# Two layer norms moved into the blocks behind them, a first pair of slabs taken chunk by chunk, a residual flipped in the experts' block, single steps ahead of double ones

## The chip, the core and the metric

The kernel runs on one core of a Trainium2 chip, as one program. The metric is the device time in microseconds (us) of an execution, the median of the runs. TensorE (PE in the profile) multiplies, VectorE (DVE) and ScalarE (ACT) work elementwise, GpSimd (POOL) does elementwise work and gathers, SyncE (SP) and ACT issue DMAs.

## The reference

Tokens are 512 rows of width 1024. A first block (attention, a convolution, a product-key expert layer) is followed by a second block of two layers, and only the second block is touched:

```python
for layer in range(2):
    sh1, sc1, g1, sh2, sc2, g2 = jnp.split(cond @ ada_w[layer] + ada_b[layer], 6, axis=-1)
    u = x * (1.0 + sc1) + sh1
    mix = _mixer(u, ...)                    # u @ w_in, short conv, gated linear attention, @ w_out
    x = _layernorm(ALPHA * x + (1.0 + g1) * mix, ln1_g[layer], ln1_b[layer])
    u = x * (1.0 + sc2) + sh2
    ff = _dense_swiglu(u, ...) if layer == 0 else _moe_swiglu(u, ...)   # 8 experts, top 2
    x = _layernorm(ALPHA * x + (1.0 + g2) * ff, ln2_g[layer], ln2_b[layer])
```

A layer norm subtracts the mean over the 1024 channels, divides by the root of the mean square plus 1e-5, and applies a gain and a bias.

## The kernel before

`x` lies with channels on the partitions: 8 chunks (`KT`) of 128 channels by 512 tokens. `self.h` holds the modulated input `u`, `self.squares` is a scratch tile of the same size. Every stage is a block of its own: all engines meet at its end. PSUM is eight banks, `bank` (four, for products) and `side` (four).

Products are made precise by splitting float32 operands in a rounded part and a rest: three matmuls for one. A weight slab of 128 output channels comes by DMA into a ring of four slots; ACT rounds it (`round_slab`, L249, two buffers, so slab i waits until slab i-2 is used), GpSimd subtracts (`split_slabs`, L257), and `fine` (L278) makes 8 chunks x 3 matmuls. The input is split the same way, ACT rounding (`round_source`, L267) and DVE subtracting (`split_source`, L272), chunk by chunk; the first slab waits for each chunk (`ready`).

`normalise` (L309) is a block: DVE centres with a mean that TensorE summed with a matrix of ones, ACT squares, TensorE sums the squares, ACT takes the root, DVE the reciprocal (L354) and scales (L357), and ACT makes `x` and then `h` of each chunk (L343). It stands after the residual of layer 0 (L2611, ahead of `dense_up`) and after `dense_down` (L2634, ahead of the second `mix_in`). The first has its mean from `residual` (L1649), which adds the chunks on DVE (L1689) and sums the result once on TensorE (L1663); the second makes eight mean matmuls itself (L365). `route` (L1828), behind the second residual, has its norm built in: gain and modulation are folded in `s.fold` (L1934 to L1936), so that `h` comes straight from the scaled `x` (L1913) and `x` gets its own gain and bias later (L1917).

`mix_in` (L1410) starts with a low-rank product of `h` with 16 columns (L1425), whose result ACT copies (L1463) ahead of its loop over slabs; then 24 slabs. `dense_up` (L1696) makes 44 slabs. `dense_down` (L1751) makes 16 wide ones, while DVE makes dot products of modulation rows (L397) that ACT fetches, and at its end the modulation's gains (`second_gains`).

`route` picks two experts for each token, turns `h` to rows (`flip`, L1859) and stores them as `token_rows`, and turns and stores ALPHA times `x` as `kept_x` (L1905, L1849), which `finish` reads back. `run_experts` (L2050) runs 15 blocks of 128 token slots as 4 double steps (two blocks of one expert) and 7 single ones. Each step streams the 33 slabs (1 MB each) of its expert, with 11 ring slots and 3 rounded buffers; some ring slots lie over `h`, `squares` and `x`. A block's rows are gathered by GpSimd into the one tile `s.xs` (L2120), turned by TensorE (L2138) and split by DVE in two halves (L2269, L2271); the next gather waits until this block is turned. Order of steps: four times (double, single), then three singles (`tail`). Two blocks are turned ahead of the loop, the others within steps (`flips`). SP issues slabs in order; the one of index `kept_over` (5), whose slot lies over `kept_x`'s source, waits for the stores.

## Time and profile before

| | us |
|---|---|
| median of 3 runs | 4841.65 (4836.25 to 4850.41) |
| the profiled run | 4848.16 |
| its span | 4846.3 |
| TensorE busy | 4079.7 (84%) |
| VectorE busy | 2875.5 (59%) |
| ScalarE busy | 1662.4 (34%) |
| GpSimd busy | 1418.9 (29%) |

The profile is one execution. The second block starts near 2280 us and the experts' loop at 3327 us. A busy share is an average over stages; each idle time is read with what ended it (`<-`). The granted clock of TensorE has two levels, shown as 1.00 (2.4 GHz) and 0.50 (1.2 GHz).

### The profile page before, as it was taken

The page shows a single profiled execution, that of the slowest core. Times are in us where ns is not written, and L with a number is a line of the kernel's source. Part 1 is how long each engine was busy: PE and PEld are TensorE (multiplying, and loading weights), DVE is VectorE, ACT ScalarE, POOL GpSimd, SP SyncE. Part 2 cuts the span into 40 slices and gives each one's busy share as a digit, 9 for nine tenths or more (in the row PEclk, how much of TensorE's full clock was granted, in tenths as well). Part 3 has the DMA queues.
Part 4 walks back from the last instruction along what each step waited for, and adds up shares of the span by engine and source line. Part 5 has one row for each costly group of instructions (what it writes and reads, how often), then busy time and mean ns, then how long its engine had stood idle before and what let it go on. Part 6 is the DMA issues. An engine that isn't in the chain of part 4 may idle for free. (4 is left out here: it accounts for less than half of the span.)

```text
span 4846.3 us, 43572 instructions
## 1 busy us (share of the span) xinstructions
PE 4079.7 (84%) x14930; PEld 2725.5 (56%) x14930; DVE 2875.5 (59%) x4171; ACT 1662.4 (34%) x2193; POOL 1418.9 (29%) x1231
## 2 busy tenths in 40 slices
PE   4988997986776766767978998977999999999995
PEld 3864543432322322323756875755878777787774
DVE  4886656565655665652364365454475664747886
ACT  2222402221211212212314323323364554646775
POOL 0430003666666666664413442310000000000000
PEclk7998998998999999999988999988999999999998
DMA  4225086999999999995312263206585765857995
GB/s 151 96 82 199 1 278 251 372 374 362 370 367 367 364 371 366 373 369 213 96 40 70 95 232 124 84 18 247 187 332 189 265 252 194 327 190 296 354 361 199
DMA packets 260053, 1147.99 MB, mean 237 GB/s; under 512 B 28832, under 2 KB 28832, under 8 KB 212512
## 3 DMA queue, kind: packets, MB, share of 16 engines
q0 software_dynamic: 150768, 549.00, 29.7%
q1 hardware_dynamic: 87792, 516.46, 29.5%
q10 hardware_dynamic: 21312, 80.15, 4.5%
q8 instruction: 110, 1.80, 0.1%
q14 instruction: 71, 0.58, 0.0%
HBM read 1131.33 MB, written 14.16 MB: 236 GB/s over the span
## 5 line engine op out<-in xcount | busy, mean ns | idle before, releaser
L1340 PE MATMUL psum<-row,diag 128*128 128x512 f32 x1632 | 802.4, 639 | 297.5 <-DMA row<-in_peer_v,expert 124.3
L1340 PEld LDWEIGHTS psum<-row,diag 128*128 128x128 f32 x1632 | 316.8, 203 | 771.7 <-issue 505.1
L1171 DVE CUSTOM_DVE_ANT_0 row<-row,psum 128x1024 f32<-128x1024 f32 x412 | 497.4, 1219 | 309.7 <-DMA row<-in_peer_u,expert 213.6
L1138 POOL DMA_INDIRECT row<-in_peer_u,expert x412 | 392.7, 953 | 561.9 <-DVE expert L1084 425.8
L2159 PE MATMUL psum<-exp_high,exp_xt 128*128 128x512 f32 x1320 | 527.3, 400 | 28.4 <-DVE exp_low L2275 17.3
L2159 PE MATMUL psum<-exp_high,exp_xlow 128*128 128x512 f32 x1320 | 517.7, 392 | 0.0
L2159 PE MATMUL psum<-exp_low,exp_xt 128*128 128x512 f32 x1320 | 515.7, 391 | 0.0
L1138 POOL DMA_INDIRECT row<-in_peer_v,expert x408 | 385.7, 945 | 255.8 <-issue 121.2
L1252 ACT ACTIVATE diag<-consts_sb,coef 128x128 f32<-128x128 f32 x512 | 175.2, 395 | 591.2 <-PE psum L1340 229.7
L2117 POOL COPY exp_number<-moe_slot_token 128x1 uint32 (+1 forms) x15 | 7.2, 482 | 1211.7 <-PE psum L2138 1155.9
L2159 PEld LDWEIGHTS psum<-exp_high,exp_xt 128*128 128x128 f32 x1320 | 248.9, 189 | 83.3 <-DVE exp_low L2275 17.4
L2159 PEld LDWEIGHTS psum<-exp_high,exp_xlow 128*128 128x128 f32 x1320 | 248.6, 188 | 53.9
L2159 PEld LDWEIGHTS psum<-exp_low,exp_xt 128*128 128x128 f32 x1320 | 249.2, 189 | 49.2
L2183 PE MATMUL psum<-exp_high,exp_ht 128*128 128x512 f32 x660 | 261.4, 396 | 13.2 <-DVE exp_htlow L2286 13.2
L2275 DVE TENSOR_TENSOR exp_low<-exp_wring,exp_high 128x2048 fp32r<-128x2048 f32 x99 | 225.3, 2291 | 75.9 <-ACT exp_high L2215 74.4
L2183 PE MATMUL psum<-exp_high,exp_htlow 128*128 128x512 f32 x660 | 261.2, 396 | 0.0
L2183 PE MATMUL psum<-exp_low,exp_ht 128*128 128x512 f32 x660 | 260.7, 395 | 0.0
L2215 ACT ACTIVATE exp_high<-exp_wring 128x2048 fp32r<-128x2048 f32 x99 | 188.4, 1913 | 56.3 <-PE psum L2183 46.9
L262 POOL TENSOR_TENSOR mix_low<-slab_ring,mix_high 128x1024 fp32r<-128x1024 f32 x48 | 119.3, 2486 | 237.6 <-ACT mix_high L255 237.6
L618 DVE SCALAR_TENSOR_TENSOR psum<-gpad,vectors_sb,psum 128x512 f32<-128x512 f32 x240 | 181.4, 756 | 8.6
L2275 DVE TENSOR_TENSOR exp_low<-slab_ring,exp_high 128x2048 fp32r<-128x2048 f32 x66 | 151.3, 2292 | 54.1 <-ACT exp_high L2215 53.5
L2275 DVE TENSOR_TENSOR exp_low<-h,exp_high 128x2048 fp32r<-128x2048 f32 x66 | 150.3, 2292 | 49.5 <-ACT exp_high L2215 49.0
(464 smaller groups left out, 8007.8 us busy)
## 6 DMA issues: line engine op xcount, KB each, us to landing
exp_wring<-in_moe SPq DMA_DIRECT2D x99, 1024.0 KB, 6.1
h<-in_moe SPq DMA_DIRECT2D x66, 1024.0 KB, 6.0
squares<-in_moe SPq DMA_DIRECT2D x66, 1024.0 KB, 6.5
x<-in_moe SPq DMA_DIRECT2D x66, 1024.0 KB, 6.6
slab_ring<-in_moe SPq DMA_DIRECT2D x66, 1024.0 KB, 5.8
slab_ring<-in_w_in SPq DMA_DIRECT2D x92, 512.0 KB
mix_rows<-in_ada ACTq DMA_DIRECT2D x48, 512.0 KB, 5.2
squares<-in_ada ACTq DMA_DIRECT2D x48, 512.0 KB, 6.4
```

What stands on the lines that cost most here:

```text
L262: pool.tensor_tensor(s.low[:, i % 2, :], self.ring[(base + i) % SLOTS][:, 0:D], s.high[:, i % 2, :].bitcast(F32), ALU.subtract).then_inc(s ...
L618: dve.scalar_tensor_tensor(sum_, gp[:, tap:tap + T], self.vec("conv_w", TAPS * c + tap), sum_, ALU.mult, ALU.add).then_inc(tapped.sem, 1)
L1138: pool.indirect_dma_start(out=s.row[row % ROWS], out_offset=None, in_=table, in_offset=bass.IndirectOffsetOnAxis(ap=s.expert[:, g, j:j + 1 ...
L1171: dve.tensor_tensor_reduce(at, at, tokens[g // PH], 1.0, 0.0, ALU.mult, ALU.add, s.act[:, g % 2, j:j + 1]).then_inc(row_used.sem, 1)
L1252: act.activation(s.diag[:, number % DIAGS, :], self.const("ident"), ACT.Copy, scale=s.coef[:, g % 2, j:j + 1]).then_inc(lined.sem, 1)
L1340: mm = pe.matmul(sums[:, half * T:(half + 1) * T], s.diag[:, (PTOP * g + j) % DIAGS, :], s.row[row % ROWS][:, half * T:(half + 1) * T], st ...
L2117: pool.tensor_copy(s.number[:], s.slot_token[:, ds(place, 1)]).then_inc(numbered.sem, 1)
L2159: mm = pe.matmul(self.bank[:, buffers(of, c).start + u, :], xx[:, part * KT // 2 + k, :], w[:, at], start=part == 0 and k == 0 and n == 0, ...
L2183: mm = pe.matmul(self.side[:, 2 * u + half, :], x[:, m, kk * P:(kk + 1) * P], w[:, at], start=c == 0 and kk == 0 and n == 0, stop=c == STE ...
L2215: act.activation(s.high[:, i % ROUNDED, :], s.wring[i % MOE_SLOTS], ACT.Copy).then_inc(rounded.sem, 1)
L2275: dve.tensor_tensor(s.low[:, i % ROUNDED, :], s.wring[i % MOE_SLOTS], s.high[:, i % ROUNDED, :].bitcast(F32), ALU.subtract).then_inc(split ...
```

## The change

- The two `normalise` blocks of the second block are gone. `dense_up` and the second `mix_in` do the norm themselves, as `route` does: folded gains, `h` and its rounded part both made by ACT from the scaled `x` (`norm_act`), DVE centring, scaling and splitting (`norm_dve`), TensorE summing the squares (`norm_pe`). ACT rounds the first two slabs ahead of it. `x` gets its gain and bias within the loop over slabs.
- The first two slabs are multiplied together, chunk by chunk (`fine_pair`); slabs 2 and 3 follow (`fine_rest`). In the second `mix_in` the low-rank product comes between them.
- `dense_down` sums `x` as `residual` does and calls `second_gains` ahead of its last wait.
- `route` no longer turns and stores `kept_x`; `run_experts` does at its start, with the stores on ACT's queue.
- In `run_experts` each pair of steps is (single, double), one block is turned ahead of the loop, and the first tail turns two.

```diff
+    def norm_act(self, act, s, eps, scale, bias):
+        for k in range(KT):
+            act.wait_ge(centred.sem, centred.at(k + 1))
+            act.activation(self.squares[:, k, :], self.x[:, k, :], ACT.Square).then_inc(squared.sem, 1)
+        act.wait_ge(summed.sem, summed.at(1))
+        act.activation(self.stat[:, 0, :], self.side[:, 0, :], ACT.Sqrt, bias=self.eps[eps], scale=1.0 / D).then_inc(rooted.sem, 1)
+        for k in range(KT):
+            act.wait_ge(scaled.sem, scaled.at(k + 1))
+            act.activation(self.h[:, k, :], self.x[:, k, :], ACT.Identity, scale=scale(k), bias=bias(k)).then_inc(normed.sem, 1)
+            act.activation(s.hhigh[:, k, :], self.x[:, k, :], ACT.Identity, scale=scale(k), bias=bias(k)).then_inc(rounded.sem, 1)
...
+    def norm_dve(self, dve, s, gain, bias, scale, shift):
...
+        for k in range(KT):
+            dve.scalar_tensor_tensor(self.x[:, k, :], self.side[:, 1, :], -1.0 / D, self.x[:, k, :], ALU.mult, ALU.add).then_inc(centred.sem, 1)
...
+        for k in range(KT + 1):
+            if k < KT:
+                dve.tensor_tensor(self.x[:, k, :], self.x[:, k, :], self.stat[:, 1, :], ALU.mult).then_inc(scaled.sem, 1)
+            if k:
+                dve.wait_ge(normed.sem, normed.at(k))
+                dve.wait_ge(rounded.sem, rounded.at(k))
+                dve.tensor_tensor(s.hlow[:, k - 1, :], self.h[:, k - 1, :], s.hhigh[:, k - 1, :].bitcast(F32), ALU.subtract).then_inc(split.sem, 1)
...
+    def fine_pair(self, pe, s):
...
+        pe.wait_ge(split.sem, split.at(2))
+        for k in range(KT):
+            pe.wait_ge(h_split.sem, h_split.at(k + 1))
+            at = slice(k * P, (k + 1) * P)
+            for slot in range(2):
+                for n, (w, x) in enumerate(((s.high, s.hhigh), (s.low, s.hhigh), (s.high, s.hlow))):
+                    mm = pe.matmul(self.bank[:, slot, :], w[:, slot, at], x[:, k, :], start=k == 0 and n == 0, stop=k == KT - 1 and n == 2)
+                if k == KT - 1:
+                    mm.then_inc(self.slab_used, 1)
...
@@ mix_in
+                if layer:
+                    self.norm_pe(pe)
+                    self.fine_pair(pe, s)
...
                 mm.then_inc(low.sem, 1)
-                self.slabs(pe, 0, SLOTS, self.fine(pe, s))
+                if layer:
+                    self.fine_rest(pe, s)
+                else:
+                    self.slabs(pe, 0, SLOTS, self.fine(pe, s))
...
+                    if layer and SLOTS < i <= SLOTS + KT:
+                        k = i - SLOTS - 1
+                        act.activation(self.x[:, k, :], self.x[:, k, :], ACT.Identity, scale=gain(k), bias=bias(k))
@@ dense_up
-                self.slabs(pe, 0, SLOTS, self.fine(pe, s))
+                self.norm_pe(pe)
+                self.fine_pair(pe, s)
+                self.fine_rest(pe, s)
...
-                self.round_source(act, s, self.h)
+                self.norm_act(act, s, LN_EPS, lambda k: s.fold[:, 0, k:k + 1], lambda k: s.fold[:, 1, k:k + 1])
@@ dense_down
+                pe.wait_ge(x_summed.sem, x_summed.at(KT - 1))
+                pe.matmul(self.side[:, 1, :], self.const("ones"), s.sum[:], start=True, stop=True).then_inc(averaged.sem, 1)
...
+                    if i == KT - 1:
+                        self.second_gains(dve, 1)
...
+                        dve.tensor_tensor(s.sum[:], s.sum[:] if i > 1 else self.x[:, 0, :], self.x[:, i, :], ALU.add).then_inc(x_summed.sem, 1)
@@ run_experts
-            return dict(step=2 * i, doubles=i, width=2, block=3 * i, place=[2 * i, 2 * i + 1], ring=[0, 1], flips=[(3 * i + 2, 2)])
+            return dict(step=2 * i + 1, doubles=i, width=2, block=3 * i + 1, place=[2 * i, 2 * i + 1], ring=[1, 2], flips=[(3 * i + 3, 0)])
...
+            return dict(step=2 * i, doubles=i, width=1, block=3 * i, place=[2 * DOUBLES + i], ring=[0],
+                        flips=[(3 * i + 1, 1), (3 * i + 2, 2)])
...
+                for t in range(TT):
+                    act.wait_ge(x_copied.sem, x_copied.at(TT + t + 1))
+                    act.dma_start(s.kept_x[t * P:(t + 1) * P, :], s.xn[:, t, :]).then_inc(x_kept.sem, 16)
                 for i in range(AHEAD):
                     round_slab(0, i)
...
-                for n in range(2):
-                    for half in range(2):
-                        x_half(n, n, half)
-                for i in range(AHEAD):
+                split_slab(0, 0)
+                for half in range(2):
+                    x_half(0, 0, half)
+                for i in range(1, AHEAD):
                     split_slab(0, i)
```

## Rows read from the trace of the kernel before

**Rows 1.** Windows (from:to and length, busy us and count per engine, clock, DMA, GB/s).
```profile
2529.90:2566.60 36.70, 10.80 (x19) 4.18 (x19) 16.87 (x22) 21.96 (x32) 3.02 (x2) 0.64 0.05 15
...
3327.60:4795.00 1467.40, 1424.27 (x6374) 1159.31 (x6374) 970.53 (x656) 791.91 (x634) 18.35 (x24) 1.00 0.71 262
```

**Rows 2.** Timeline (start us, us, engine, line, operation, idle before), join A.
```profile
2533.68 4.88 DVE L351 SCALAR_TENSOR_TENSOR x<-psum,x 128x512 f32<-128x512 f32 x8 [1.50 <-PEq L1653]
...
2535.09 9.64 PE L371 MATMUL psum<-squares,consts_sb 128*128 128x512 f32 x16 [1.73 <-ACT squares L330]
...
2545.48 3.35 DVE L354 RECIPROCAL stat<-stat 128x512 f32<-128x512 f32 x1 [6.93 <-ACT stat L332]
...
2576.85 1.06 ACT L255 ACTIVATE ffn_high<-slab_ring 128x1024 fp32r<-128x1024 f32 x1 [8.24 <-PE psum L290]
...
2577.99 2.40 POOL L262 TENSOR_TENSOR ffn_low<-slab_ring,ffn_high 128x1024 fp32r<-128x1024 f32 x1 [9.28 <-ACT ffn_high L255]
```

**Rows 3.** Timeline, the folded gains and the h activations in `route`.
```profile
3240.30 0.17 DVE L1934 TENSOR_TENSOR route_fold<-vectors_sb,cooked 128x8 f32<-128x8 f32 x1 [1.50 <-PEq L1653]
...
3256.49 5.77 ACT L1913 ACTIVATE h<-x,route_fold 128x512 f32<-128x512 f32 x8 [4.21 <-DVE x L1946]
```

**Rows 4.** Forms of one line (duration ns min/median/max, first to last start).
```profile
L276 DVE TENSOR_TENSOR ffn_hlow<-h,ffn_hhigh x8: 678/680/2866, 2565.0 to 2572.2; 128x512 fp32r<-128x512 f32 x8
...
L1689 DVE TENSOR_TENSOR res_sum<-res_sum,x x12: 691/2762/2762, 2503.5 to 3238.1; 128x512 f32<-128x512 f32 x12
...
L618 DVE SCALAR_TENSOR_TENSOR psum<-gpad,vectors_sb,psum x240: 755/756/760, 138.3 to 355.7; 128x512 f32<-128x512 f32 x120
```

**Rows 5.** Timeline, end of `dense_down` and start of the second `mix_in`.
```profile
2949.93 0.75 DVE L1813 TENSOR_SCALAR stat<-psum,cooked 128x512 f32<-128x512 f32 x1 [1.37 <-PE psum L1773]
...
2987.52 8.60 PE L1425 MATMUL psum<-h,small_sb 128*16 128x512 f32 x16 [17.74 <-PEq L321]
...
3002.01 1.06 ACT L255 ACTIVATE mix_high<-slab_ring 128x1024 fp32r<-128x1024 f32 x1 [5.27 <-PE psum L290]
...
3007.59 1.06 ACT L255 ACTIVATE mix_high<-slab_ring 128x1024 fp32r<-128x1024 f32 x1 [4.03 <-PE psum L290]
```

**Rows 6.** Timeline, end of `route` and start of `run_experts`.
```profile
3287.58 6.38 PE L1859 MATMUL psum<-consts_sb,x 128*128 128x128 f32 x32
...
3289.47 0.17 DVE L2025 CAST moe_slot_token<-psum 128x16 uint32<-128x16 f32 x1
...
3292.55 2.89 SPq L1849 DMA_DIRECT2D kept_x<-squares  x4
...
3295.91 0.20 ACT L2209 ACTIVATE exp_mark<-eps 128x1 f32<-128x1 f32 x1 [1.31 <-PEq L1841]
...
3297.24 0.99 POOL L2120 DMA_INDIRECT exp_xs<-token_rows,exp_number  x1 [0.77 <-POOL exp_number L2117]
...
3302.93 1.91 ACT L2215 ACTIVATE exp_high<-exp_wring 128x2048 fp32r<-128x2048 f32 x1 [6.82 <-DMA exp_wring<-in_moe]
...
3305.76 1.12 PE L2138 MATMUL psum<-consts_sb,exp_xs 128*128 128x128 f32 x4 [11.79 <-DMA exp_xs<-token_rows,exp_number]
...
3320.12 1.11 PE L2138 MATMUL psum<-consts_sb,exp_xs 128*128 128x128 f32 x4 [10.56 <-DMA exp_xs<-token_rows,exp_number]
...
3327.63 0.79 PE L2159 MATMUL psum<-exp_high,exp_xt 128*128 128x512 f32 x1 [3.71 <-DVE exp_low L2275]
```

**Rows 7.** Windows (columns as in Rows 1), most of the first double step.
```profile
3335.00:3420.00 85.00, 83.59 (x380) 68.50 (x380) 42.01 (x29) 33.51 (x25) 1.15 (x2) 1.00 0.53 188
```

**Rows 8.** Windows of TensorE alone: busy, clock, DMA share, GB/s.
```profile
3327.60:3332.00 4.40, 4.37 (x10) 0.50 1.02 425
...
3577.70:3581.20 3.50, 3.50 (x10) 0.52 0.96 405
```

**Rows 9.** Timeline, TensorE waits for a gather inside single steps.
```profile
3577.14 0.65 PE L2138 MATMUL psum<-consts_sb,exp_xs 128*128 128x128 f32 x4 [2.66 <-DMA exp_xs<-token_rows,exp_number]
...
4456.02 0.65 PE L2138 MATMUL psum<-consts_sb,exp_xs 128*128 128x128 f32 x4 [0.94 <-DMA exp_xs<-token_rows,exp_number]
```

141 lines of the change are left out of this document (90 added, 51 removed).

## The prediction

> **What bounds the kernel now.** I read the windows of the two long stretches first. In the experts' loop TensorE is busy 1424 of 1467 us at full clock, so nothing the other engines save inside the loop is worth anything; only when it starts, and what TensorE waits for in it, counts [rows 1]. In the first join, from the last product of the residual to the first of the dense layer, TensorE is busy 10.8 of 36.7 us at a mean clock of 0.64 [rows 1]. The change works on three such joins, called A (into `dense_up`), B (into the second `mix_in`) and C (into `run_experts`). In the timelines the reader is to follow which engine releases which.
>
> **Join A, the chain before.** Centring starts at 2533.68, the sum of squares takes TensorE 9.64 us because its clock is low at first, Sqrt takes 0.75 us between the sum and the reciprocal, the reciprocal 3.35 [rows 2]; then scaling and sixteen activations, a block end, two slab roundings, the split of h, and products from 2566.6 [rows 1]. Slab 0 is used at 2576.85 and slab 1 a slab time of 5.58 later (the spacing of the two roundings in [rows 5]), so slab 2 starts at 2582.4.
>
> **Join A, after.** The block starts at the same 2533.7. DVE folds gains (three operations of 0.17, 0.5 with gaps [rows 3]) and centres. ACT has two slab roundings ahead of its squares (1.06 each by [rows 2], 2.0), so the first square starts at 2535.7 and the TensorE sum some 0.7 later, 2536.4; with 9.64 it ends 2546.1. Sqrt 0.75 and reciprocal 3.35 give 2550.2. Then the first chunk passes scale 0.68, two activations at 0.72 spacing (eight in 5.77, [rows 3]) and the subtraction 0.68 [rows 4], about 3.1 with latencies: the pair begins at 2553.3. Later chunks come every 1.45 to 1.5 us (two activations; DVE needs 1.3), below the 2.56 that six matmuls take at low clock and near the 1.40 at full clock (5.58/24 each). 48 matmuls: about 10 in 4.4 us at low clock, as at the loop's start [rows 8], and 38 x 0.2325 = 8.8; end 2566.5. The moved affine of x (eight times 0.72) lies on ACT beside 5.58 us slabs of which ACT uses under 3: cost nothing; without that cover it would be 0.7 per chunk. The split of h loses its one blocked operation (2.87 against 0.68, [rows 4]), since GpSimd is done by then; that is already in the sum.
>
> Something is given back. Both slabs of the pair finish within three matmuls, and slab 2's rounding waits for slab 0's use, at 2565.8: rounding and split take 3.54 (2576.85 to the end of the GpSimd row, [rows 2]), so slab 2 starts at 2569.5 and TensorE idles 3.0. A wait of 2.66 in the loop was followed by 3.5 us at half clock [rows 8, 9], a loss of 1.75; I take 1.8 here, between 0 and 2.2. A = 2582.4 - 2569.5 - 1.8 = **11.1 us**.
>
> **Join B.** Before, slab 1 of `mix_in` is used at 3007.6 [rows 5]. After, `dense_down` sums x itself: seven DVE additions and one TensorE product in place of eight matmuls. The additions are on an engine that waits for TensorE at the end (1.37, [rows 5]). One that overlaps GpSimd takes 2.76 instead of 0.69 [rows 4], but now the row dot that was caught there is not, so each costs 0.7; `second_gains` (five operations on a few columns, 0.6 by the 0.17 of [rows 3] with overlap) moves ahead of the last wait, and what is queued behind it is the last x chunk. 1.37 covers 0.7 + 0.6; without the cover up to 1.5. From the last product to centring I take join A's 2533.7 - 2529.9 = 3.8: block start 2953.6. The same 19.6 to the pair gives 2973.2, and 13.2 more 2986.4. Then comes the low-rank product, now behind the pair: 8.60 before, partly at low clock; sixteen passes at 0.427 are 6.8, so I take 6.9 (ends 6.8 and 8.6). The ACT wait for it stands ahead of `next_slab(0)`, so queued behind it are its copy (0.6), the rounding of slab 2 and GpSimd's split: 2993.3 + 0.6 + 3.54 + 0.1 = 2997.5. Gain 10.1, less 2.2 for the clock after 4.2 idle (4.4 at half speed, [rows 8]): B = **7.9 us**.
>
> **Join C.** The route block loses eight transposed tiles, their copies and four stores. It ended with ACT, whose idle of 1.31 began at 3294.6; now DVE's cast at 3289.47 + 0.17 ends it [rows 6]: 5.0 sooner. Everything in the new block shifts so: the gather is issued at 3292.2 and, with the first one's 8.5 (3297.24 to the flip that waited for it at 3305.76), lands at 3300.7. TensorE flips x first (6.38, ACT ending 7.0 after its start [rows 6]) from 3290.9 to 3297.9, beside the wait for the gather. ACT then issues four stores (at most 0.72 each by SP's row, which holds waits for copies [rows 6]; 1.7 taken) and rounds slab 0 at 3299.7, which arrives at 3302.93 - 5.0 = 3297.9. Queued behind these waits on ACT are the first three roundings; on SP the slab of index 5 and everything behind it wait until the stores have landed. DVE splits slab 0 (2.3) to 3304.0, then does two halves of block 0, with a flip between, by 3308.2. TensorE starts there instead of at 3327.63, which waited for a second gather until 3320.12 [rows 6]: 19.4. At 425 GB/s [rows 8] a 1 MB slab takes 2.5 us and the stores' 2 MB take 5.0; slab 5 is issued by 3308.5, lands by 3316 and is wanted at about 3322, so this wait is hidden by 6 us. The single step lasts about 99 us (33 slabs x 12 products x 0.2325 = 92, and transposes), near 3.0 a slab, slower than 2.5, so a ring that starts empty holds. One block's flips move from ahead of the loop into the first tail: two flips of 0.6, plus a gather wait of 0 to 2.66 and the clock after it [rows 9]; I take the wait of 0.94 at 4456, the nearest row in time and in DMA load: 2.1 in all. C = 19.4 - 2.1 = **17.3 us**. With the stores' 5.0 lost, a wait of 2.66 and its 1.75 of clock it is 8.8, without any wait 18.2.
>
> The Trainium skill's SBUF page ("SBUF — State Buffer", section "SBUF: two separate sides") says that a DVE operation with two SBUF inputs and a GpSimd operation that reads SBUF lock each other out for a whole instruction. It speaks against the added additions in `dense_down`, and the trace agrees (0.69 or 2.76, [rows 4]). By it centring, which has one input in PSUM, would escape GpSimd's two splits, as the rows of L618 show (755 to 760 ns beside GpSimd). The page on DMA ("DMA: Bandwidth & Descriptors", section "Queues, rings and completion order") says that queues take turns by packet. By that, the stores on ACT's queue halve the slabs' rate for 10 us; slab 2 would come at 3308.7 and be split by 3313, where TensorE wants it at 3315.8, so the sum stays. No run here shows those two queues so loaded.
>
> **The sum.** 11.1 + 7.9 + 17.3 = 36.3 us. The profiled run took 4848.16, its span is 4846.3, so the changed one's should be near 4811.9 and 4810.0. The median of the three runs is 6.5 lower, 4841.65, which gives **4805.4 us**.
>
> **Rivals.** (1) Locks and clock eat the joins. GpSimd's two splits (5.1) now run beside centring; if they block it, 5.1 is lost in each join, and if low clock lasts twice its 4.4, since TensorE works with gaps there, 2.2 more. A is 3.8, B 0.6: 21.7 in all, 4820.0. Against it: L618 [rows 4]. (2) The experts' start collides: the stores hold back slab 0 or the gather by their full 5.0, and the first tail pays a full wait and half clock, 2.66 + 1.75. C is 8.8, the sum 27.8, time 4813.9. For it: ACT's 6.82 wait for slab 0 [rows 6] shows that it comes little before it is wanted. (3) The pair doesn't pay: chunk order only moves the wait to slab 2 and to the low-rank product. Then each join saves eight activations (5.7) and C its block end (5.0): 16.4, 4825.3. (4) Slower: the first step, a single one on an empty ring, is bound by slabs. In the first double step DMA moved 188 GB/s [rows 7]; at that rate 33 slabs take 184 us instead of 99, which is +85.1 - 36.3 = +48.8, 4890.5. It cancels the gain from 255 GB/s down. Against it: that rate was what the ring asked for (DMA share 0.53); before it the rate was 425.
>
> **Chances.** Forecast 0.63 (its own range 4796 to 4814), (1) 0.15, (2) 0.13, (3) 0.05, (4) 0.04. The bounds of the terms give gains of 3.8 + 0.6 + 8.8 = 13.2 up to 12.9 + 10.1 + 18.2 = 41.2, 4800 to 4828; the three runs spread over 14 us, so I set 4794 to 4826. About 0.3% (14.5 us) is what a measurement of this kernel can tell from none. Faster 0.88 (a bit of (1) to (3) falls past 4827), same 0.08, slower 0.04.
>
> **What would show it.** In A the first product of the pair at 2553, slab 2 at 2569 to 2571, an idle of 3 us ahead of it with GpSimd's split as its releaser, then half clock for some 4 us. In B the low-rank product starting near 2986 and an idle of 4 behind it. In C the first expert matmul 18.6 us behind route's last cast where it was 38.0, one gather ahead of it, SP waiting for the stores, no ACT wait for slabs after the third. A first step over 105 us, or centring with a 2.8 us operation, would prove (4) or (1); a gather wait over 2 us in the first tail, (2).

## The result, and the profile after

The changed kernel takes 4803.63 us (median of 5 runs, 4799.84 to 4813.17) where the kernel before takes 4841.65: ratio 0.9923, 95% interval 0.9907 to 0.9939, or 38.0 us less. The forecast was 4805.4. The profiled run took 4799.84, its span is 4798.0. The two profiled spans differ by 48.3, but 12.6 of that had been gained ahead of the first changed line (the last product of the residual ends at 2517.4 where it ended at 2530.0, in code that is the same), so the profiles are compared stretch by stretch. Each is one execution, and the next section shows which stretches come out otherwise in other profiles. In the changed kernel the norm's lines are L390 to L425, the pair L438, the low-rank product L1498, the single flip of `x` L2291.

| stretch, us | before | after | gain | forecast |
|---|---|---|---|---|
| A: residual's last TENSOR_SCALAR to the first rounding of `dense_down` | 290.6 | 279.8 | 10.8 | 11.1 |
| `dense_down`, to its last TENSOR_SCALAR | 129.4 | 129.5 | -0.1 | 0 |
| B: from there to the second residual's last TENSOR_SCALAR | 286.7 | 276.2 | 10.5 | 7.9 |
| `route`: from there to its last cast | 52.9 | 52.8 | 0.1 | 0 |
| C: cast to the first expert matmul | 38.2 | 18.7 | 19.5 | 19.4 |
| experts' loop, to its last copy from PSUM | 1467.9 | 1472.5 | -4.6 | -2.1 |

Windows of the changed kernel (from:to and length, busy us and count per engine, clock, DMA share, GB/s): join A up to the pair, the pair with the idle behind it, the start of slab 2, the start of slab 2 in join B, and the loop. They answer to [rows 1, 8].

```profile
2517.40:2541.70 24.30, 11.84 (x18) 4.36 (x19) 12.79 (x19) 9.29 (x15) 4.70 (x2) 0.69 0.07 22
2541.70:2558.70 17.00, 13.98 (x48) 10.84 (x48) 8.32 (x13) 12.84 (x17) 2.34 (x1) 0.83 0.14 47
2558.70:2562.70 4.00, 3.96 (x17) 3.27 (x18) 2.50 (x1) 1.52 (x3) 2.40 (x1) 1.00 0.18 69
2973.70:2977.30 3.60, 3.59 (x9) 2.91 (x10) 3.53 (x3) 0.00 (x0) 2.63 (x1) 0.54 0.02 5
3274.40:4746.40 1472.00, 1429.37 (x6382) 1163.20 (x6382) 972.72 (x660) 791.62 (x634) 20.61 (x27) 0.99 0.71 267
```

Before, 36.7 us passed from the residual to the first product; now it is 24.3. The third and fourth windows each stand behind an idle time of TensorE, and they differ: full clock in A, 0.54 in B.

The timeline of join A after the change (start us, us, engine, line, operation, idle before and its releaser), for [rows 2]:

```profile
2522.11 4.87 DVE L407 SCALAR_TENSOR_TENSOR x<-psum,x 128x512 f32<-128x512 f32 x8
2524.30 10.09 PE L425 MATMUL psum<-squares,consts_sb 128*128 128x512 f32 x16 [2.88 <-ACT squares L390]
2535.14 3.35 DVE L409 RECIPROCAL stat<-stat 128x512 f32<-128x512 f32 x1 [8.17 <-ACT stat L392]
2541.71 0.77 PE L438 MATMUL psum<-ffn_hhigh,ffn_high 128*128 128x512 f32 x1 [7.33 <-DVE ffn_hlow L418]
2555.12 1.06 ACT L255 ACTIVATE ffn_high<-slab_ring 128x1024 fp32r<-128x1024 f32 x1 [4.08 <-PE psum L438]
2556.25 2.34 POOL L262 TENSOR_TENSOR ffn_low<-slab_ring,ffn_high 128x1024 fp32r<-128x1024 f32 x1 [28.70 <-ACT ffn_high L255]
2558.74 0.47 PE L290 MATMUL psum<-ffn_hhigh,ffn_high 128*128 128x512 f32 x1 [3.05 <-POOL ffn_low L262]
```

ACT can't round slab 2 before the pair has used slab 0, at 2555.1; then ACT and GpSimd take 3.5 us, and TensorE idles 3.05 of it. Join B shows the same with the low-rank product and its copy ahead of the rounding, for [rows 5]:

```profile
2962.54 7.04 PE L1498 MATMUL psum<-h,small_sb 128*16 128x512 f32 x16
2969.61 0.59 ACT L1542 ACTIVATE low_rank<-psum 16x512 f32<-16x512 f32 x1 [10.99 <-PE psum L1498]
2970.11 1.04 ACT L255 ACTIVATE mix_high<-slab_ring 128x1024 fp32r<-128x1024 f32 x1
2971.22 5.11 POOL L262 TENSOR_TENSOR mix_low<-slab_ring,mix_high 128x1024 fp32r<-128x1024 f32 x2 [34.73 <-ACT mix_high L255]
2973.71 0.50 PE L290 MATMUL psum<-mix_hhigh,mix_high 128*128 128x512 f32 x1 [4.14 <-POOL mix_low L262]
```

The experts' start, for [rows 6]: one gather ahead of the first matmul, and SP's slab issues, which stop at 3260.4 for the stores issued by ACT at 3262.9 and go on only at 3281.86.

```profile
3255.70 0.17 DVE L2111 CAST moe_slot_token<-psum 128x16 uint32<-128x16 f32 x1
3257.72 0.98 POOL L2208 DMA_INDIRECT exp_xs<-token_rows,exp_number  x1 [0.78 <-POOL exp_number L2205]
3260.10 0.33 SPq L2191 DMA_DIRECT2D h<-in_moe  x1
3262.88 3.02 ACTq L2352 DMA_DIRECT2D kept_x<-squares  x4
3268.13 1.11 PE L2226 MATMUL psum<-consts_sb,exp_xs 128*128 128x128 f32 x4 [5.29 <-DMA exp_xs<-token_rows,exp_number]
3274.41 0.79 PE L2247 MATMUL psum<-exp_high,exp_xt 128*128 128x512 f32 x1 [1.60 <-DVE exp_xlow L2372]
3281.86 0.92 SPq L2191 DMA_DIRECT2D squares<-in_moe  x2
```

What nobody forecast is at the edge of the loop. With single steps first, the end of each double step and the start of the next single step lie on the two sides of the edge. The first edge:

```profile
3574.64 0.59 ACT L2318 ACTIVATE cond_rows<-psum 128x512 f32<-128x512 f32 x1
3576.21 1.28 ACT L2337 ACT_TABLE_LOAD   x1 [0.98 <-ACT cond_rows L2318]
3577.78 3.70 ACT L2309 ACTIVATE exp_high<-h 128x2048 fp32r<-128x2048 f32 x2
3582.07 0.80 PE L2247 MATMUL psum<-exp_high,exp_xt 128*128 128x512 f32 x1 [3.03 <-DVE exp_low L2376]
```

ACT loads a function table at the head of the loop body, and the rounding behind it is what TensorE waits for through DVE. The waits at the three edges are 3.03, 3.02 and 2.85, and each is followed by about half clock (windows of TensorE alone: busy, clock, DMA share, GB/s):

```profile
3582.00:3585.50 3.50, 3.43 (x9) 0.57 0.61 208
3875.20:3878.70 3.50, 3.42 (x8) 0.52 0.64 220
4168.60:4172.10 3.50, 3.41 (x8) 0.51 0.56 208
```

### The profile page after: what moved, and what is told of

Its sections match the earlier page's. It is cut to its first block and busy times, and to the rows that moved or that the text cites. A ratio compares the mean times of both kernels' runs of the same rounds, so it can differ in the third digit from the quotient of the medians.

```text
span 4798.0 us, 43540 instructions
## 1 busy us (share of the span) xinstructions
PE 4081.0 (85%) x14916; PEld 2727.2 (57%) x14916; DVE 2873.6 (60%) x4184; ACT 1659.6 (35%) x2193; POOL 1416.2 (30%) x1231
## 5 line engine op out<-in xcount | busy, mean ns | idle before, releaser
L2271 PE MATMUL psum<-exp_high,exp_ht 128*128 128x512 f32 x660 | 261.5, 396 | 13.2 <-DVE exp_htlow L2387 13.2
L1410 PE MATMUL psum<-stat,diag 128*128 128x512 f32 x204 | 116.5, 699 | 83.0 <-DMA stat<-in_peer_v,expert 39.4
L2376 DVE TENSOR_TENSOR exp_low<-slab_ring,exp_high 128x2048 fp32r<-128x2048 f32 x66 | 151.2, 2291 | 52.9 <-ACT exp_high L2309 52.3
```

What stands on the lines that cost most here:

```text
L1410: mm = pe.matmul(sums[:, half * T:(half + 1) * T], s.diag[:, (PTOP * g + j) % DIAGS, :], s.row[row % ROWS][:, half * T:(half + 1) * T], st ...
L2271: mm = pe.matmul(self.side[:, 2 * u + half, :], x[:, m, kk * P:(kk + 1) * P], w[:, at], start=c == 0 and kk == 0 and n == 0, stop=c == STE ...
L2376: dve.tensor_tensor(s.low[:, i % ROUNDED, :], s.wring[i % MOE_SLOTS], s.high[:, i % ROUNDED, :].bitcast(F32), ALU.subtract).then_inc(split ...
```

## The experiments

The twelve kernels ran on three chips, whose own medians of the kernel before are 4717.86 (e1 to e4), 4850.24 (e5 to e8) and 4857.41 (e9 to e12). Times are compared within a chip; no profile of the kernel before was taken on any of the three, so its stretches are those of the table above and, where a kernel leaves them as they were, those of e1 to e3. The stretches were read in each profile (d: `dense_down`, to its last TENSOR_SCALAR; r: `route`, to its last cast):

| kernel | median, ratio (interval) | A | d | B | r | cast to first matmul | loop |
|---|---|---|---|---|---|---|---|
| e1 join A only | 4707.81, 0.9976 (0.9966 to 0.9987) | 277.7 | 129.4 | 286.1 | 52.8 | 38.2 | 1474.4 |
| e2 join B only | 4708.85, 0.998 (0.9969 to 0.999) | 290.3 | 130.6 | 276.6 | 53.7 | 38.6 | 1474.9 |
| e3 join C only | 4694.91, 0.9946 (0.9929 to 0.9963) | 289.3 | 129.2 | 286.5 | 52.8 | 18.1 | 1473.8 |
| e4 slabs one by one | 4685.80, 0.9928 (0.9911 to 0.9944) | 277.6 | 130.2 | 281.7 | 55.9 | 18.6 | 1476.0 |
| e5 the change again | 4815.18, 0.9929 (0.9913 to 0.9946) | 278.9 | 130.6 | 276.6 | 53.7 | 18.9 | 1473.5 |
| e6 series, early rounding | 4814.38, 0.9923 (0.9907 to 0.994) | 277.6 | 130.9 | 274.5 | 55.9 | 18.7 | 1474.7 |
| e7 loop written out | 4806.86, 0.9908 (0.9891 to 0.9924) | 277.6 | 130.3 | 278.0 | 52.9 | 18.4 | 1469.6 |
| e8 double steps first | 4822.72, 0.9948 (0.9931 to 0.9964) | 278.9 | 130.2 | 276.9 | 54.9 | 32.6 | 1467.3 |
| e9 low-rank wait later | 4813.99, 0.9915 (0.9897 to 0.9934) | 277.6 | 130.4 | 271.6 | 55.9 | 18.1 | 1475.8 |
| e10 flip later | 4808.81, 0.9902 (0.9884 to 0.9921) | 278.9 | 130.2 | 277.0 | 54.9 | 18.2 | 1463.6 |
| e11 stores' slots last | 4820.12, 0.9924 (0.9906 to 0.9943) | 277.6 | 130.9 | 277.5 | 52.9 | 18.7 | 1472.6 |
| e12 all of it | 4795.72, 0.988 (0.9861 to 0.9899) | 277.7 | 130.9 | 270.7 | 55.8 | 18.4 | 1456.8 |

Two columns move without having been meant to. `dense_down` ends at 129.2 to 129.4 with its old code (before, e1, e3), at 129.5 in the first profile of the change, and at 130.2 to 130.9 in the ten other kernels that have its new code. And `route` takes 52.8 to 55.9, though it is the same code in all but e1 and e2, which have that of before. Both are taken up below.

### One join at a time (e1, e2, e3)

Each has the functions of one join from the change (e1 `dense_up`; e2 `dense_down` and `mix_in`; e3 `route` and `run_experts`) and the others from before, with their `normalise` blocks back. Against the change, e2 and e3 have at join A

```diff
+                    self.normalise(self.x, T, LN_EPS, [(self.x, ACT.Identity, vec("ln1_g"), vec("ln1_b")),
+                                                       (self.h, ACT.Identity, column(self.cooked, 5), mod2(3, 0))], centre=True, averages=False)
```

> Only the norm in front of dense_up (join A) is moved and its first two slabs paired; join B and the experts are as in the kernel before. Theory: the three parts are separate stretches and add up; in the two profiles A gave 10.8 us (from the residual's last TENSOR_SCALAR to the first down_high rounding, 290.60 before and 279.81 after), so this kernel is 10.8 us faster than before (4831, ratio 0.9978) and the later stretches, from down_high on, have the durations of the kernel before: 129.4 in dense_down, 286.7 in mix_in, 1467 in the expert loop. Rival (the joins depend on each other through the clock or the order of the slabs): the stretch of A is again 279.8, but the sum over all three single-part kernels differs from the 38.0 of the whole change by over 3 us, and the missing time stands in a later stretch of this kernel.

> Only the norm in front of mix_in of layer 1 (join B) is moved and its first two slabs paired. Theory: residual to residual takes 276.2 us for 286.7 and the run is 10.5 us faster than before (4831, ratio 0.9978). Rival (the gain of B that went beyond the predicted 7.9 is run-to-run spread of the long mix_in stretch and no work of the change): the stretch comes out at 278.8 (286.7 less 7.9) or the slab-2 start at +47.0 us is not met again.

> Only the start and the order of the experts (join C) is changed; both norms are as before. Theory: last cast to first expert matmul 18.7 us for 38.2, the loop 4.6 longer (1472.0 for 1467.4), so 14.9 faster than before (4827, ratio 0.9969), with waits of about 3 us on exp_low at each entry of a pair of steps, each followed by half clock. Rival (the joins ahead decide the state in which the experts start, for instance how far the slab stream is ahead): the 18.7 or the loop's 4.6 differ by over 1 us from those of the full change.

Measured: 10.1, 9.0 and 23.0 us below 4717.86, 42.1 together. Each stretch has its changed length only where its join is changed: A 277.7 for 289.3 and 290.3, B 276.6 for 286.1 and 286.5, the start 18.1 for 38.2 and 38.6. So each join's own stretch doesn't depend on the others, and they are worth about 12, 10 and 20. Three expectations missed. e3 was to gain 14.9 and gained 23.0: on this chip the loop isn't longer with single steps first (1473.8 for 1474.4 and 1474.9), so the 4.6 us lost there in the first pair of profiles is no fixed price of the order; nor was each wait at an edge followed by half clock (behind the first, of 3.09 us, it was 1.00). In e2 slab 2 starts at +48.8 us and not at +47.0, one of the two signs named for its rival, though B is 276.6 as the theory had it. And the sum is 4.1 off the 38.0 of the whole change, where the rival in e1 asked for over 3; the intervals of the three ratios are 10 to 16 us wide each, so the medians can't decide that.

### Is it the pair? (e4, e5, e6, e9)

In e4 slabs 0 and 1 are multiplied one after the other, still chunk by chunk:

```diff
@@ dense_up
-                self.fine_pair(pe, s)
-                self.fine_rest(pe, s)
+                self.slabs(pe, 0, SLOTS, self.fine(pe, s))
@@ mix_in
-                    self.fine_pair(pe, s)
+                    pe.wait_ge(h_split.sem, h_split.at(KT))
...
-                    self.fine_rest(pe, s)
+                self.slabs(pe, 0, SLOTS, self.fine(pe, s))
```

> The whole change, but both joins multiply slab 0 and slab 1 one after the other over all chunks, with the product of the norm's ones matrix still merged into the block and mix_in's low-rank product ahead of slab 0. Theory: slab 0 can then not start before the last chunk of h is scaled and split, so TensorE waits for all eight chunks: the pair's start at +24 us becomes about +36 to +38 for slab 0 alone (the pair ended at +38.3 in A and had two slabs behind it), slab 2 starts some 7 us later at each join, and the kernel loses about 14 us against the change (4818, ratio 0.995 against before). Rival (the pair is what costs: chunk by chunk at half clock and in step with DVE it takes as long as waiting and then running both slabs at full rate): slab 2 starts within 1.5 us of +41.3 and +47.0, and the time is within 3 us of the change.

Missed for A: it is 277.6, as with the pair. My theory overlooked that the first slab waits for each chunk by itself, with or without the pair. The timeline of e4, times 2395.8 for the residual's last TENSOR_SCALAR:

```profile
2418.42 0.77 PE L290 MATMUL psum<-ffn_hhigh,ffn_high 128*128 128x512 f32 x1 [7.33 <-DVE ffn_hlow L418]
...
2424.24 0.50 PE L290 MATMUL psum<-ffn_hhigh,ffn_high 128*128 128x512 f32 x1 [0.58 <-DVE ffn_hlow L418]
...
2429.68 1.06 ACT L255 ACTIVATE ffn_high<-slab_ring 128x1024 fp32r<-128x1024 f32 x1 [1.93 <-PE psum L290]
2430.82 2.39 POOL L262 TENSOR_TENSOR ffn_low<-slab_ring,ffn_high 128x1024 fp32r<-128x1024 f32 x1 [25.02 <-ACT ffn_high L255]
```

Slab 0 starts at +22.6 in both, takes 11 us in step with DVE (gaps of 0.4 to 0.6), and its rounded buffer is free at 2429.7; slab 2 is ready at 2433.2, under slab 1, and TensorE goes on to it without an idle at +39.2. With the pair (e1) slab 2 starts at +39.2 too, behind an idle of 3.04. The pair fills the gaps between chunks and pays the same time at slab 2. At B e4 loses 5.0 (281.7 for the 276.6 of e2), but there the low-rank product stands ahead of slab 0 and waits for all chunks, which the next kernels take apart. The median is 32.1 us below before; this chip has no run of the change to set beside it.

> The changed kernel itself on the chip of these runs, as the base for the three beside it. The parts measured alone gave 10.1, 9.0 and 23.0 us, 42.1 together. Theory (the parts are independent): about 42 us faster than before here, ratio near 0.991, with stretches A 277.7, B 276.6, cast to first expert matmul 18 to 18.7 and the same 24.3 / 47.0 marks as in the first profile, within a microsecond of clock. Rival (they interact): the sum is missed by over 4 us.

Measured 35.1 us and 0.9929, beside 38.0 and 0.9923 in the first measurement. The 42.1 of the parts is missed by 7, more than the rival's 4, but the interval of e5 alone is 26 to 42 us. In the profiles A, B and the start together take 574.3 us, for 572.4 alone. Where the 7 us are isn't shown: the loop of the old order took 1467.9 in the profile of before and 1474.4 and 1474.9 in e1 and e2, a difference of that size, but there is no profile of before on this chip. Of the marks, the pair starts at +23.5 at A (24.3 expected), and slab 2 at B at +48.75 (47.0 expected, a miss). It is at +48.2 to +49.1 in all six kernels here that have this join as changed (e2, e5, e7, e8, e10, e11); the +47.0 of the first profile didn't come again.

e6 takes slab 0, the low-rank product, slab 1, slab 2, and has ACT round slab 2 ahead of the low-rank copy. e9 keeps the pair and has that last edit alone:

```diff
-                act.wait_ge(low.sem, low.at(1))
-                act.activation(s.low_rank[0:16, :], self.side[0:16, 0, :], ACT.Copy).then_inc(low.sem, 1)
+                def low_copy():
+                    act.wait_ge(low.sem, low.at(1))
+                    act.activation(s.low_rank[0:16, :], self.side[0:16, 0, :], ACT.Copy).then_inc(low.sem, 1)
+                if not layer:
+                    low_copy()
                 for i in range(QK):
                     next_slab(i)
+                    if layer and i == 0:
+                        low_copy()
```

> No pair: at join A slab 0 goes chunk by chunk in step with DVE, then slab 1, then slab 2; at join B slab 0, the low-rank product, slab 1, slab 2, and ACT rounds slab 2 ahead of its copy of the low-rank result. Theory (the pair only shifts the wait to slab 2, because both rounded buffers come free at once; in series the rounding of slab 2 runs beside slab 1): A as with the pair, 277.6 for 277.7. At B slab 0 ends near +35.3, low-rank product 6.9, slab 1 5.6, so slab 2 starts near +47.9 where it was +48.8 with an idle of 4.1 and half clock behind it; B is 0.9 plus 1.7 shorter, about 274.0, and no idle over 1 us stands ahead of slab 2. Against the change about 2.6 us faster. Rival (the pair pays at B, as the run without a pair, 5.0 us longer there, could mean): B comes out at 277 or more.

> The change with one thing moved: in the second mix_in ACT rounds slab 2 ahead of its wait for the low-rank product instead of behind it. Theory (at join B the idle of 4.1 us ahead of slab 2 is ACT queueing behind the low-rank wait, not the pair): rounding starts when the pair ends, near +37.5 from the last TENSOR_SCALAR of dense_down, and is done with its split near +41, under the low-rank product, so slab 2 starts as that ends, at +44.7 for +48.75, and the half clock behind the idle is gone: B 5 to 5.8 us shorter (271 for 276.6), which is also 2 to 3 shorter than without the pair (274.45). Rival (POOL or another user of the queue is what is late): slab 2 stays near +48, or the gain is given back later in mix_in.

In the stretch both are as expected: B is 274.5 in e6 and 271.6 in e9, for 276.6 in e5 and for 277.0 and 277.5 in e10 and e11, the kernels of e9's chip. The timeline of e9 shows slab 2 rounded and split under the low-rank product, and TensorE going straight on:

```profile
2976.58 1.06 ACT L255 ACTIVATE mix_high<-slab_ring 128x1024 fp32r<-128x1024 f32 x1 [3.66 <-PE psum L438]
2977.72 2.35 POOL L262 TENSOR_TENSOR mix_low<-slab_ring,mix_high 128x1024 fp32r<-128x1024 f32 x1 [27.48 <-ACT mix_high L255]
2979.67 4.45 PE L1498 MATMUL psum<-h,small_sb 128*16 128x512 f32 x10
2984.06 0.50 PE L290 MATMUL psum<-mix_hhigh,mix_high 128*128 128x512 f32 x1
```

But `route` behind it gives some of this back: it takes 55.9 us in both, for 53.7 in e5. Its code is the same, and TensorE's clock is lower there. The same 25 us in e5 and then in e6, from 20 us behind the residual's last TENSOR_SCALAR:

```profile
3236.20:3261.20 25.00, 23.39 (x124) 0.57 0.04 15
```

```profile
3232.30:3257.30 25.00, 24.21 (x114) 0.50 0.00 1
```

B and `route` together take 330.3 in e5, 330.3 in e6 and 327.4 in e9, and the median of e6 is 0.8 us below that of e5. So against slabs in series the pair as placed gives and costs nothing up to the cast, and once something covers the rounding behind it, it is worth 2.9 (327.4 for 330.3). `route` takes 55.8 to 55.9 in all four kernels without an idle ahead of slab 2 in B (e4, e6, e9, e12) and 52.8 to 54.9 in all others; why isn't shown.

### Is it the loop's edge? (e7, e8)

e7 replaces the loop over the four pairs by written-out code on all five engines:

```diff
-                with pe.Fori(0, DOUBLES) as i:
+                for i in range(DOUBLES):
```

> The change with the experts' four loop passes written out, so no engine has a loop edge. Theory (the wait of 2.85 to 3.1 us for exp_low at the entry of each later single step comes from the loop edge: ACT loads its function table again there, 1.28 us, ahead of its rounding, and TensorE's clock falls after the wait): without the edge these three waits are 1.67 as at the last, unlooped single step, no half clock follows, and each is 1.3 plus 1.7 cheaper: the loop stretch is about 9 us shorter (1463 to 1467 for 1472 to 1476) apart from gather waits. Rival 1 (the wait is DVE's or the slabs' and has nothing to do with the edge): the waits stay near 3. Rival 2 (code loading of the written-out steps costs more than the edges): new waits by issue stand in the steps.

Mostly as expected: the loop stretch is 1469.6 and not 1463 to 1467, but with four gather waits in it (3.20, 1.19, 2.43 and 1.61 us, with a clock of 0.60 and 0.57 behind the first and third), where e5 has 2.67 and 1.67 and three under 0.5. That is 3.2 us of waits more than in e5 and one fall of the clock more, some 1.6; without them the loop would be 8.7 shorter than in e5 (9 expected). This last figure is an estimate. The median is 8.3 us below e5, and no new wait by issue stands in the steps. The waits at the entries of the three later single steps, in e7's timeline:

```profile
3593.61 0.50 PE L2247 MATMUL psum<-exp_high,exp_xt 128*128 128x512 f32 x1 [1.66 <-DVE exp_low L2376]
3885.21 0.50 PE L2247 MATMUL psum<-exp_high,exp_xt 128*128 128x512 f32 x1 [1.66 <-DVE exp_low L2376]
4175.57 0.50 PE L2247 MATMUL psum<-exp_high,exp_xt 128*128 128x512 f32 x1 [1.67 <-DVE exp_low L2376]
```

The clock behind all three is 1.00. A single step without a gather wait takes 97.1 us for 99.9 to 100.3 behind an edge in the change. The double steps take 193.27 for 193.35, so writing out costs nothing. The table load is gone at all three (the one ahead of the first pass stays), but that it alone makes the 1.4 us of each wait isn't shown, since the edge's branch went with it.

e8 undoes the order: double steps first and two blocks turned ahead, all else as in the change.

```diff
-                    step(single(i))
                     step(double(i))
+                    step(single(i))
...
-                split_slab(0, 0)
-                for half in range(2):
-                    x_half(0, 0, half)
-                for i in range(1, AHEAD):
+                for n in range(2):
+                    for half in range(2):
+                        x_half(n, n, half)
+                for i in range(AHEAD):
```

> The change with double steps first again and two blocks turned ahead of the loop; kept_x is still turned and stored in the experts' block. Theory: of the 19.5 to 20 us by which the experts start sooner, 5.0 come from the route block's earlier end and the rest from needing one block instead of two, so cast to first expert matmul is about 33; the waits at the step entries move back (1.67 at the entry of singles, about 2 by issue hidden at the entry of doubles), so the loop is 3 x 1.3 or some 4 us shorter than in the change, apart from gather waits: 10 to 11 us slower than the change in all. Rival (the loop of the change isn't longer by its order, the differences are gather waits that vary from run to run): the loop is within 1.5 us of that of the change once gather waits and the low clock behind them are taken off. Other rival (the stores beside the slabs hold back the second gather or slabs): the start is over 36.

The start takes 32.6 us (33 expected): 13.7 of the change's gain come from needing one block instead of two, 5.6 from the earlier end of `route`. The median is 7.5 us above e5 (10 to 11 expected): the loop took 1467.3, 6.1 shorter than in e5 where 4 were expected. The 4 was worked out from an edge that costs the double steps nothing, and it costs here too: the double steps behind it take 194.4, 196.3 and 196.5 us, against 193.3 where no edge is ahead. The windows of TensorE behind the three edges:

```profile
3592.60:3596.10 3.50, 3.50 (x16) 1.00 0.95 316
3884.10:3887.60 3.50, 3.50 (x11) 0.68 0.91 315
4178.80:4182.30 3.50, 3.50 (x9) 0.52 0.98 337
```

So the edge costs 1.1 where the clock stays up and 3.0 to 3.3 where it falls.

### Is it the gathers and the stores? (e10, e11)

The flips of a single step stand at chunks 2, 5, 6 and 9 of its 11; the second block's gather is issued once the first is turned, at 5. e10 moves one flip:

```diff
-            return {2 * n + 2 + half: (q, ring, half % 2) for n, (q, ring, half) in enumerate((q, ring, half) for q, ring in of["flips"] for half in range(2))}
+            return {(2, 5, 7, 9)[n]: (q, ring, half % 2) for n, (q, ring, half) in enumerate((q, ring, half) for q, ring in of["flips"] for half in range(2))}
```

> The change with one flip of each single step moved one slot later: the first half of the second block is turned at chunk 7 in place of 6, so its gather has two chunks (17.6 us) instead of one (8.8) between issue and use. Theory (what varies the loop between 1467 and 1476 us is this gather, which takes just over 8.8 beside the slabs): all waits for exp_xs by DMA inside single steps are gone; the first step is 103 to 104 us for 107, the first tail 97 for 98.7, the others as they were without a gather wait; the loop about 6 us shorter than the 1473.5 of the change. The three waits of 3 us on exp_low at the entry of single steps stay. Rival (the gather is late because its queue is starved, not because it is issued late): waits of 1 to 3 us remain at the later slot.

Measured: no wait for a gather is left, the first step takes 102.7 us (107.5 in e5), the first tail 96.7 (98.7), the loop 1463.6, 9.9 less than in e5, where 6 were expected; the median is 11.3 us below e11, the kernel of the same chip whose loop is that of the change but for the ring's order. Some of the extra is the clock. The windows of TensorE behind the three edge waits of e10, which were 3.02, 2.98 and 3.03 us long:

```profile
3597.40:3600.90 3.50, 3.50 (x9) 0.57 0.65 225
3890.30:3893.80 3.50, 3.48 (x10) 0.66 0.63 215
4183.20:4186.70 3.50, 3.46 (x15) 1.00 0.68 214
```

The steps behind them take 99.7, 99.6 and 98.0 us: with the longest of the waits the clock didn't fall, and the step is 1.6 shorter.

e11 has the two ring slots over the stores' source last of the eleven:

```diff
+                        if i == s.x_over:
+                            sp.wait_ge(x_flipped.sem, x_flipped.at(FLIPS))
...
-                    s.wring += [flat(tile[:, 4 * j:4 * j + 4, :]) for tile in (self.h, self.squares, self.x) for j in range(2)]
-                    s.kept_over = MOE_SLOTS - 8 + 2
+                    s.wring += [flat(tile[:, 4 * j:4 * j + 4, :]) for tile in (self.h, self.x) for j in range(2)]
+                    s.x_over, s.kept_over = MOE_SLOTS - 8 + 2, MOE_SLOTS - 2
                     s.wring += [self.slab_ring[:, j * KT * FC:(j + 1) * KT * FC] for j in range(2)]
+                    s.wring += [flat(self.squares[:, 4 * j:4 * j + 4, :]) for j in range(2)]
```

> The change with the two ring slots over the source of kept_x made the last of the eleven, so that SP waits for the four stores at slab 9 instead of slab 5 (slots over x wait only until x is turned). Theory (the wait of SP for the stores, 21 us and until 25 us behind the block's start, is long but hidden, since the slabs landed before it feed TensorE until the ring catches up): the SP wait shrinks below 10 us, no TensorE wait changes, the cast to the first expert matmul and the first step stay within 0.5 us, and the time is within 1 us of the change. Rival (the late slab 5 costs: it delays slabs 6 to 10 and with them the first step and its gather): the first step is 2 us or more shorter than the 107.

SP's wait is 17.8 us, not under 10: with four more slabs issued ahead, the stores have landed 21 us after the first was issued, where it was 19. The rest is as expected, a start of 18.7, a first step of 106.9 and a loop of 1472.6; the ratio, 0.9924, can't be told from the change's 0.9923 and 0.9929. The wait is long and hidden.

### All together (e12)

At A slab 1 now follows slab 0 by four chunks, so that slab 0 is done first; the rest are the edits of e7, e9, e10 and e11:

```diff
+        for turn in range(KT + lag):
+            for slot in range(2):
+                k = turn - lag * slot
+                if not 0 <= k < KT:
+                    continue
```

> All of it together: the late low-rank wait at join B, the later flip, the stores' ring slots last, the experts' loop written out, and at join A a staggered pair in which slab 1 follows slab 0 by four chunks, so that slab 0 ends some 3 us sooner and the rounding of slab 2 runs beside the end of slab 1. Theory (the leftovers are separate): against the change 5.4 at B, 2 to 2.5 at A (idle ahead of slab 2 from 3.0 to under 1), 9 by the loop edges, 4 to 6 by the gather waits, 20 to 22 us in all; against before 54 to 60, ratio 0.988. Rival (at A DVE and ACT pace the chunks, and the staggered order only trades the idle at slab 2 for gaps between chunks): A within 0.5 us of the pair, the rest as said.

It is the fastest kernel: 4795.72 us, 61.7 below before and 24.4 below e11. Not all of that is its work: of the 28.0 us between the profiles of e11 and e12, 8.9 lie ahead of the first changed line. Behind it the stretches give about 20, the lower end of what was expected: the loop 15.8 (1456.8), B 6.8 (270.7), less 2.9 that `route` takes longer. At A the idle ahead of slab 2 is 0.28 us:

```profile
2569.93 0.47 PE L290 MATMUL psum<-ffn_hhigh,ffn_high 128*128 128x512 f32 x1 [0.28 <-POOL ffn_low L262]
```

From the first product of the pair to slab 2 pass 14.9 us, for 16.5 to 17.0 in the kernels with the plain pair. Yet A itself is 277.7, within 0.5 of theirs, which was the rival's sign: the chain ahead of the pair took 24.3 us in this run, as in the first profile of the change, and 22.6 in e1, e4, e7 and e9. The sum of squares in it takes 10.1 us in the first two and 8.5 to 9.1 in the others. So the 1.6 to 2.1 us of the staggered order are seen ahead of slab 2 and not in the whole stretch.

## Why the prediction was right, and where its steps were not

The total was right partly by luck. In the first pair of profiles the stretches add up to 36.2 us (10.8 - 0.1 + 10.5 + 0.1 + 19.5 - 4.6) for the 36.3 forecast, but by errors of -0.3 at A, +2.6 at B and -2.4 at C that cancel. The medians give 38.0 with an interval of 29.5 to 45.0, too wide to tell one such error.

**Join A** (11.1 forecast, 10.8 measured, 11.6 and 12.6 in e1 beside e3 and e2). The chain went as worked out, centring without a lock, Sqrt, reciprocal, eight chunks. The pair began at +24.3 from the residual's last TENSOR_SCALAR in the first profile (23.3 forecast), as the sum of squares began 0.5 later and took 10.09 us for the 9.64 of [rows 2]; it lasted 14.0 (13.2 forecast). The idle of 3.0 came with GpSimd's split as its releaser: 3.05. So slab 2 came 1.8 late, at +41.3. The mis-sized term is the clock behind it: 1.8 taken, 0 measured. The two errors cancel by chance. The step that named the 2.66 of [rows 9] as a pattern failed, since the clock doesn't follow the length of the wait.

**Join B** (7.9 forecast, 10.5 measured). The pair at +22.6 (23.3), the low-rank product 7.04 (6.9), the idle 4.14 (4.2), half clock behind it (0.54 over 3.6 us, about 1.7 for the 2.2 taken), slab 2 at +47.0 (47.6), all in the first profile; in the kernels after it the pair starts at +23.4 to +24.2 and slab 2 at +48.2 to +49.1. Up to the first products of the attention, the gain is 8.7. The other 1.7 is one product, the same in both kernels, that found a higher clock. In the profile of before and then of after:

```profile
3139.89 8.86 PE L1569 MATMUL psum<-gv,squares 128*128 128x256 f32 x32 [2.12 <-DVE a L1604]
```

```profile
3107.93 7.17 PE L1656 MATMUL psum<-gv,squares 128*128 128x256 f32 x32 [2.12 <-DVE a L1691]
```

It took 8.86 again in e3 and 7.17 in e1, both with B as before, so it isn't bound to the change. That doesn't make it spread that can be taken off: e1 came to it 1.3 us later and its B is 286.1 all the same, and B is 276.2 to 278.0 in all seven kernels that have this join as changed. A gain of 8.1 to 10.5 for the 7.9 repeats; why it is more isn't shown.

The added sums in `dense_down` were costed too low. I took 0.7 us each; by the timeline six of seven take 3.6, the lock that [rows 4] show, under TensorE's products, and the last, the one on the path, is 0.69:

```profile
2913.10 3.62 DVE L1917 TENSOR_TENSOR down_sum<-down_sum,x 128x512 f32<-128x512 f32 x1
2928.20 0.69 DVE L1917 TENSOR_TENSOR down_sum<-down_sum,x 128x512 f32<-128x512 f32 x1
```

In this profile that was hidden, with `dense_down` at 129.5. In the ten others it wasn't, and the forecast's term of nothing for the moved gains is the one that failed: DVE's last dot product waits 2.6 to 4.1 us for its row of modulation, `second_gains` now stands behind that and ahead of the last chunk of `x`, and the last TENSOR_SCALAR comes 1.1 to 2.3 us behind TensorE's last product, for 0.1 to 0.4 with the old code. In e5:

```profile
2937.83 1.23 DVE L467 CUSTOM_DVE_ANT_0 squares<-squares,cond_rows 128x1024 f32<-128x1024 f32 x1 [3.47 <-DMA squares<-in_ada]
...
2939.34 0.39 DVE L488 TENSOR_SCALAR cooked<-mod 128x8 f32<-128x8 f32 x4
2939.64 0.74 DVE L1910 TENSOR_SCALAR stat<-psum,cooked 128x512 f32<-128x512 f32 x1
```

The last product had ended at 2938.1. So `dense_down` is 0.8 to 1.8 us longer than with the old code; for this case the prediction had named up to 1.5.

**Join C** (17.3 forecast, 14.9 measured). Cast to first matmul, 18.6 forecast, was 18.7; of the 5.0 for the block's end e8 shows 5.6. Failed steps: (a) the issue of slab 5, forecast 17.6 us behind the block's start, came at 25.4, as the stores had landed 19 us after the first was issued and not some 10. (The four issues on ACT, for which 1.7 was taken, took 3.0.) It was hidden nonetheless (e11), so the sum stands. (b) The "2.1 in all" for the loop was 4.6. The forecast put a gather wait in the first tail, and it came (1.81), but gathers had cost before as well (2.66, 1.37, 0.24 and 0.94, now 2.49, two of 0.2 and 1.81). What isn't in the sum at all is the edge of the loop. Before, the double steps behind the edges took 194.4, 194.5 and 195.0; now the single ones do, with 99.9, 100.1 and 99.9. Against the 193.3 and 96.9 that e12 shows without edges, that is 9.2 us for 4.1. By e8 and e10 the difference, some 1.7 us an edge, is whether the clock falls behind the wait, and it falls in either order; over all profiles the loop took 1467.3 to 1474.9 with double steps first (four) and 1472.5 to 1476.0 with single steps first, edge and flips as changed (seven).

**The rivals.** (1) Locks: centring's eight operations took 4.87 and 4.86 us beside GpSimd's 4.7 in the two joins, as L618 had shown. By the Trainium skill's page "SBUF — State Buffer", section "SBUF: two separate sides", a DVE operation with two SBUF inputs and a GpSimd operation that reads SBUF lock each other out; the trace agrees, with 0.6 each for L407 (one input in PSUM) and 3.6 for L1917 (both in SBUF). (2) A colliding start: cast to first matmul 18.7, and no wait of TensorE for a late slab in the first step; the gather wait in the first tail was 1.81, at full clock. (4) A starved first step: 106.9 us, not 184. (3), "the pair doesn't pay", had 5 in 100 and was half right: at A the pair gives nothing (e4), and at B, as placed, nothing up to the cast (e6). But its price was wrong by far, since the chunk-by-chunk start that I had put down to the pair comes with the merged norm, whose `h` is ready chunk by chunk and which the first slab alone takes as it comes. So the total was right with one of its reasons credited wrongly.

## What to carry to other kernels

When two units of work share the wait for their input, look at what comes behind them: if both free their buffers at once, the gain is handed to the next unit, and it is kept only where other work covers the refill or where one of the two is let finish first. A wait placed ahead of an unrelated step on a busy queue (ACT's wait for the low-rank product ahead of a rounding) and an input fetched one unit ahead of its use (the gather) cost 5 to 6 us of B (e9; 3 of them up to the cast) and up to 9.9 us of the loop (e10). Before moving an operation ahead of a wait, ask whether it waits for something later itself: `second_gains` did, for a DMA. Before moving work across a loop's edge, read what each engine does at the edge, and compare a stretch, and the one behind it, in more than one profile: the loop in its old order took 1468 us in one profile and 1474 and 1475 in two others, and what e6 gained in one stretch it lost in the next.

## What the runs showed of the hardware

- TensorE's clock falls from 2.4 to 1.2 GHz behind some idle times and not behind others of the same length: behind the 4.13 to 4.14 us in B it fell in all seven kernels that have this idle (0.54 to 0.62), behind the 3.04 to 3.05 in A in none of the eight that have this idle, and behind three idle times of 2.98 to 3.03 us in e10 it fell twice. It fell behind 1.82 us in e8 (0.68) and not behind 3.09 in e3 (1.00). Behind the waits of 1.66 and 1.67 in e7 and e12 it stayed up all six times. A fall costs about 1.6 us (99.7 and 99.6 for 98.0 in e10).
- A loop's edge isn't free of work on ACT: a table load of 1.28 us stands at the head of every pass of the loop body, in both orders, though each pass uses the same functions; written out (e7, e12), only the first is left.
- Four stores of 0.5 MB beside a stream of slabs on another queue had landed 19 us after the first was issued, and 21 with four more slabs ahead (e11). In the changed kernel's window from 3263 to 3281, with the 16 DMA engines over 0.9 busy, the queue of the slabs (q1) and that of the stores (q10) moved (packets, MB, share of 16 engines):

```profile
q1 hardware_dynamic: 530, 3.82, 53.4%
q10 hardware_dynamic: 575, 2.10, 28.5%
```

  The Trainium skill's page "DMA: Bandwidth & Descriptors", section "Queues, rings and completion order", says that queues take turns by packet; these nearly equal counts agree, if the profile's packets are the page's, which no run here shows. What failed is the prediction's step from turns to an even split of the bytes (10 us): a packet of the stores held 3.7 KB on average and one of the slabs 7.2.
